# Two fused blocks on one core: the second block's first two tiles from undivided x, scans ahead of taps, one weight pass in four parts

## What is computed

```python
# end of the first block
x = x + ga2 * ((silu(gate) * up) @ w_down)
x = rmsnorm(x, g_final)
# the second block
h = rmsnorm_2(x, norm_g) * (1 + scale) + shift
cv, cg, cs, lx, ls = split(h @ w_in)          # 5 times 1024 columns
v = cv * sigmoid(cg)
v = causal_depthwise_conv(v, dw_w, dw_b)      # 31 taps a channel
v = silu(layernorm(v, cln_g, cln_b)) @ pw2_w + pw2_b
y_conv = v * silu(cs)
xs = causal_depthwise_conv(lx, sc_w, sc_b)    # 4 taps a channel
r = sigmoid(xs @ wr + br); i = sigmoid(xs @ wi + bi)      # by head
a = exp(-8 * r * softplus(-lam)); bx = sqrt(1 - a * a) * (i * xs)
hs = linear_scan(a, bx)                       # h = a h + bx along the tokens
x = x + (1 + gate) * (concat([y_conv, hs * silu(ls)]) @ w_out)
out = rmsnorm_2(x, final_g)
```

## Time and profile before

| | us |
|---|---|
| median of 3 runs | 1064.8 (1064.68 to 1064.96) |
| the profiled execution | 1064.87 |
| its span in the profile | 1063.1 |
| busy: TensorE | 1037.2 (98%) |
| busy: VectorE | 629.8 (59%) |
| busy: GpSimd | 471.5 (44%) |
| busy: ScalarE | 421.6 (40%) |
| mean granted TensorE clock | 0.998 |

### The profile page before, as it was taken

The page is one execution under the profiler, slowest core; times in us unless marked ns, Lnnn a source line. Parts: engine busy times, 40 slices in busy tenths (PEclk is TensorE's granted clock), DMA queues, the critical chain, the costliest instruction groups (busy, mean ns, idle before and its releaser), DMA issues.

```text
span 1063.1 us, 14023 instructions
## 1 busy us (share of the span) xinstructions
PE 1037.2 (98%) x5222; PEld 836.4 (79%) x5222; DVE 629.8 (59%) x1223; ACT 421.6 (40%) x585; POOL 471.5 (44%) x173
## 2 busy tenths in 40 slices
PE   6999999999999999999999999999999999999997
PEld 5787796667878888888888888888887777888886
DVE  5367997776463432224347100779999999664322
ACT  4244325883242222122242312424526777362242
POOL 0034343592333443534434444256865666734350
PEclk9999999999999999999999999999999999999999
DMA  9984231140424345343473323224231222322312
GB/s 325 349 288 126 73 117 40 41 160 1 158 80 158 118 133 178 124 157 119 133 237 124 109 85 105 80 80 158 79 119 40 79 80 80 119 80 93 105 40 80
DMA packets 127250, 128.91 MB, mean 121 GB/s; under 512 B 3552, under 2 KB 125280, under 8 KB 127200
## 3 DMA queue, kind: packets, MB, share of 16 engines
q1 hardware_dynamic: 125952, 127.38, 37.0%
q10 hardware_dynamic: 1248, 0.86, 0.3%
HBM read 126.13 MB, written 2.10 MB: 121 GB/s over the span
## 4 chain that ended last, share of the span: by engine, by line
PE 45%; issue 35%; POOL 14%; ACT 2%; SPq 1%; DMA 1%; DVE 1%; POOLq 0%; DVEq 0%; ACTq 0%
POOL w_lo L589 12%; PE bank L704 9%; PE bank L706 9%; PE bank L705 9%; PE bank L1021 2%; PE bank L1050 2%; PE bank L893 2%; PE bank L1245 1%; PE bank L1246 1%; PE bank L1244 1%; DMA ada_stage<-in_w_ada 1%; POOL lru_lo L682 1%; PE bank L911 1%; PE bank L729 1%; PE bank L730 1%
## 5 line engine op out<-in xcount | busy, mean ns | idle before, releaser
L589 POOL TENSOR_TENSOR w_lo<-w_stage,w_hi 128x2048 fp32r<-128x2048 f32 x78 | 371.5, 4762 | 500.4 <-ACT w_hi L1315 500.4
L704 PE MATMUL bank<-act_hi,w_hi 128*128 128x512 f32 x848 | 335.3, 395 | 1.2 <-POOL w_lo L589 1.1
L705 PE MATMUL bank<-act_lo,w_hi 128*128 128x512 f32 x848 | 330.0, 389 | 0.0
L706 PE MATMUL bank<-act_hi,w_lo 128*128 128x512 f32 x848 | 330.0, 389 | 0.0
L1315 ACT ACTIVATE w_hi<-w_stage 128x2048 fp32r<-128x2048 f32 x78 | 149.3, 1915 | 247.3 <-PE bank L706 236.1
L704 PEld LDWEIGHTS bank<-act_hi,w_hi 128*128 128x128 f32 x848 | 159.3, 188 | 40.1 <-issue 5.6
L706 PEld LDWEIGHTS bank<-act_hi,w_lo 128*128 128x128 f32 x848 | 159.2, 188 | 33.5
L705 PEld LDWEIGHTS bank<-act_lo,w_hi 128*128 128x128 f32 x848 | 159.3, 188 | 33.1 <-issue 1.2
L2156 DVE SCALAR_TENSOR_TENSOR bank<-v_pad,vcol,bank 128x512 f32<-128x512 f32 x208 | 138.1, 747 | 0.0
L2068 DVE TENSOR_TENSOR tmp<-bank,tmp 128x512 f32<-128x512 f32 x22 | 15.2, 692 | 157.1 <-PE bank L706 153.6
L704 PE MATMUL bank<-ff_hi,w_hi 128*128 128x512 f32 x176 | 69.7, 396 | 0.0
(11 more groups left out here) (316 smaller groups left out, 1548.1 us busy)
## 6 DMA issues: line engine op xcount, KB each, us to landing
w_stage<-in_w_in SPq DMA_DIRECT2D x29, 1024.0 KB, 5.1
w_stage<-in_w_gu SPq DMA_DIRECT2D x22, 1024.0 KB, 5.1
ada_stage<-in_w_ada SPq DMA_DIRECT2D x20, 1024.0 KB, 11.6
w_stage<-in_w_out SPq DMA_DIRECT2D x12, 1024.0 KB, 5.1
ada_stage<-in_mod_w SPq DMA_DIRECT2D x12, 1024.0 KB, 7.6
w_stage<-in_w_down SPq DMA_DIRECT2D x8, 1024.0 KB, 5.3
late_stage<-in_w_ada SPq DMA_DIRECT2D x4, 1024.0 KB, 9.4
w_stage<-in_pw_w SPq DMA_DIRECT2D x4, 1024.0 KB, 5.1
```

What stands on the lines that cost most here:

```text
L589: nc.gpsimd.tensor_tensor(w_lo[b][:], w_stage[b][:], w_hi[b][:].bitcast(F32), ALU.subtract).then_inc(s_lo, 1)
L704: pe.matmul(dst, wh, rhs_hi(k), start=(first and k == 0), stop=False)
L705: pe.matmul(dst, wh, rhs_lo(k), start=False, stop=False)
L706: mm = pe.matmul(dst, wl, rhs_hi(k), start=False, stop=(last and k == n_k - 1))
```

## The change

*Undivided tiles.* After each residual tile ScalarE makes `act_hi` and VectorE `act_lo` of xT times `scale1`, without the norm and the shift; TensorE runs the first chunk's two tiles on them, partly between the square sums. VectorE multiplies the two results by the inverse norm, and a sigmoid adds the bias row: the shift times the weights of that chunk, summed by VectorE over k (`bias_rows`) and by TensorE over the partitions, 128 columns at a time. The normed parts are still made, for the third tile on, and each waits until its undivided part is used. The sum of the square rows takes bank 2 in place of 0, and the filler matmuls there go.
*First block's output.* The eight VectorE products by g_final and the norm go; ScalarE copies the spread norm to SBUF, multiplies xT by g_final, and GpSimd by the norm, two tiles behind each of four chunks.
*Taps.* `TAPS_B` 10, 10, 10, 18 become 6, 6, 6, 10.
*w_lo in four.* Chunk C_OUT+1's pass is four passes over 512 columns each.
Beside these, SP waits for the bias rows before it loads chunk C_IN2+2 (they read the stage), and some semaphores are shared.

```diff
-TAPS_A, TAPS_B = (10, 10, 10, 10), (10, 10, 10, 18)
+TAPS_A, TAPS_B = (10, 10, 10, 10), (6, 6, 6, 10)
...
+            w_dma(C_IN2, w_cols(a["w_in_2"], 0, KD, D))
+            w_dma(C_IN2 + 1, w_cols(a["w_in_2"], 0, KD, 0))
+            sp.wait_ge(s_adaacc, len(ADA_ORD) + 1)
...
+            def lo_quarters(n, b):
+                pool.wait_ge(s_hi, n + 1)
+                for q in range(4):
+                    ks = slice(2 * q, 2 * q + 2)
+                    i = nc.gpsimd.tensor_tensor(w_lo[b][:, ks, :], w_stage[b][:, ks, :], w_hi[b][:, ks, :].bitcast(F32), ALU.subtract)
+                i.then_inc(s_lo, 1)
...
+                if n == C_OUT + 1:
+                    lo_quarters(n, n % 2)
+                    continue
...
+                if n in (C_IN2 + 4, C_IN2 + 6, C_IN2 + 8, C_IN2 + 10):
+                    for k in range(n - C_IN2 - 4, n - C_IN2 - 2):
+                        pool.wait_ge(s_x1g, k + 2)
+                        nc.gpsimd.tensor_tensor(xT[:, k, :], xT[:, k, :], cgate[:, 0, :], ALU.mult).then_inc(s_x1, 1)
...
                 if meanwhile:
                     meanwhile()
+                    if gained:
+                        spread(6, 7)
                     if spreads_back:
                         spread(4, 5)
                     return
                 keep_warm(WARM_COLUMNS, idle)
-                if gained:
-                    spread(6, 7)
...
+                        if (m2, g, m) == (KD // 2 - 1, 2, 0):
+                            pe.wait_ge(s_adaacc, len(ADA_ORD) + 1)
+                            for c in range(2):
+                                mm = pe.matmul(bank[7][:, NCOL + c:NCOL + c + 1], ada2_acc[:, c * P:(c + 1) * P], ones[:, 0:1],
+                                               start=True, stop=True)
+                            mm.then_inc(s_adamm, 1)
+            def undivided(ks):
+                for k in ks:
+                    pe.wait_ge(s_rawlo, k + 1)
+                    for dst, cols, ready in ((bank[0][:], low, s_i2acc), (bank[1][:], high, s_wused)):
...
+            def first_undivided():
+                pe.wait_ge(s_lo, C_IN2 + 1)
+                pe.wait_ge(s_res, 2 * KD - 2)
+                undivided((0, 1))
+
+            square_sums(gained=True, before=first_undivided, meanwhile=lambda: undivided((2, 3)))
+            undivided(range(4, KD))
             pe.wait_ge(s_res, 2 * KD)
             pe.wait_ge(s_lo, C_IN2 + 2)
-            abreast(third, 2, range(KD // 4))
-            abreast(two, 2, range(KD // 2, KD))
-            abreast(third, 2, range(KD // 4, KD))
-            tile(bank[3][:], b1, high, KD, hi, lo).then_inc(s_wused, 1)
+            abreast([(bank[2][:], b1, low, s_i2acc), (bank[3][:], b1, high, s_wused)], 2)
...
+                    if held and k < KD - 1:
+                        act.wait_ge(s_rawused, k + 1)
+                    elif held:
+                        act.wait_ge(s_wused, C_IN2 + 1)
...
+            def undivided_high(k):
+                if k == 0:
+                    act.wait_ge(s_mod, 11)
+                nc.scalar.activation(act_hi[:, k, :], xT[:, k, :], ACT.Copy, scale=scale1[:, 0, k:k + 1]).then_inc(s_rawhi, 1)
...
+                if j == 1:
+                    act.wait_ge(s_spread, 4)
+                    nc.scalar.activation(cgate[:, 0, :], bank[4][:], ACT.Copy).then_inc(s_x1g, 1)
+                    for k in range(KD):
+                        act.wait_ge(s_u, 2 * KD + k + 1)
+                        nc.scalar.activation(xT[:, k, :], xT[:, k, :], ACT.Copy, scale=col("g_final", k)).then_inc(s_x1g, 1)
...
+                            if j == 0:
+                                act.wait_ge(s_div, m + 1)
+                                act.wait_ge(s_mod, 12)
+                                nc.scalar.activation(tmp[m][:], tmp[m][:], ACT.Sigmoid, bias=first_bias[:, m:m + 1]).then_inc(s_sig, 1)
+                                continue
...
+            def bias_rows():
+                dve.wait_ge(s_stage[C_IN2 % 2], C_IN2 // 2 * 16 + 16)
+                for t in range(KD):
+                    src, w, part = w_stage[C_IN2 % 2][:, t, :], modc(SH3 + t), bank[7][:, 0:NCOL]
...
+                    if gained and k == KD - 2:
+                        bias_rows()
+                    if gained and k == KD - 1:
+                        dve.wait_ge(s_adamm, len(ADA_ORD) + 1)
+                        V.tensor_copy(first_bias[:], bank[7][:, NCOL:NCOL + 2]).then_inc(s_mod, 1)
                     if k >= 1:
                         add_squares(k - 1, gained)
+                    if gained and k >= 1:
+                        dve.wait_ge(s_rawhi, k)
+                        V.scalar_tensor_tensor(act_lo[:, k - 1, :], xT[:, k - 1, :], scale1[:, 0, k - 1:k],
+                                               act_hi[:, k - 1, :].bitcast(F32), ALU.mult, ALU.subtract).then_inc(s_rawlo, 1)
...
             normed(0, SH3, bank[6], (5, 7))
-            dve.wait_ge(s_spread, 4)
-            dve.wait_ge(s_u, 3 * KD)
-            for k in range(KD):
-                V.scalar_tensor_tensor(xT[:, k, :], xT[:, k, :], col("g_final", k), bank[4][:], ALU.mult, ALU.mult).then_inc(s_x1, 1)
-
+            link(V.tensor_copy(rstd[:], bank[6][:]))
+            for m in range(2):
+                dve.wait_ge((s_i2acc, s_wused)[m], (1, C_IN2 + 1)[m])
+                V.tensor_tensor(tmp[m][:], bank[m][:], rstd[:], ALU.mult).then_inc(s_div, 1)
```

More of the change, by code:

```diff
@@ L313, in build @@
         s_adaloop = sem("ada_loop_loaded")
-        s_late_ada = [sem(f"late_ada_loaded{b}") for b in range(len(ADA_LATE))]
         s_adastep = sem("ada_step")
@@ L337, in build @@
         s_sdg = sem("gained_deviation_ready")
+        s_rawhi = sem("undivided_hi_ready")
+        s_rawlo = sem("undivided_lo_ready")
+        s_rawused = sem("undivided_parts_used")
+        s_div = sem("first_tiles_divided")
         s_rc = sem("inverse_columns_ready")
@@ L561, in _ @@
                     late_dma(2 * n - 2)
-            stream(C_IN2, 4, [lambda j: w_cols(a["w_in_2"], 0, KD, j * NCOL + (D - NCOL)),
-                              lambda j: w_cols(a["w_in_2"], 0, KD, j * NCOL - NCOL)], first=1)
+            w_dma(C_IN2, w_cols(a["w_in_2"], 0, KD, D))
+            w_dma(C_IN2 + 1, w_cols(a["w_in_2"], 0, KD, 0))
+            sp.wait_ge(s_adaacc, len(ADA_ORD) + 1)
+            stream(C_IN2 + 2, 3, [lambda j: w_cols(a["w_in_2"], 0, KD, j * NCOL + (D - NCOL)),
+                                  lambda j: w_cols(a["w_in_2"], 0, KD, j * NCOL - NCOL)], first=2)
             for g in range(2):
@@ L752, in sums @@
                     return mm
-                plain = 0 if gained else 6
+                plain = 2 if gained else 6
                 if gained:
@@ L1172, in _ @@
                             late_products(b)
-            square_sums(gained=True)
+                        if (m2, g, m) == (KD // 2 - 1, 2, 0):
[4 more added lines that the diff above has]
+                            mm.then_inc(s_adamm, 1)
+            b0, b1 = C_IN2 % 2, (C_IN2 + 1) % 2
+            def undivided(ks):
+                for k in ks:
+                    pe.wait_ge(s_rawlo, k + 1)
+                    for dst, cols, ready in ((bank[0][:], low, s_i2acc), (bank[1][:], high, s_wused)):
+                        wh, wl = w_hi[b0][:, k, cols], w_lo[b0][:, k, cols]
+                        pe.matmul(dst, wh, act_hi[:, k, :], start=(k == 0), stop=False)
+                        pe.matmul(dst, wh, act_lo[:, k, :], start=False, stop=False)
+                        mm = pe.matmul(dst, wl, act_hi[:, k, :], start=False, stop=(k == KD - 1))
+                        if k == KD - 1:
+                            mm.then_inc(ready, 1)
+                    if k < KD - 1:
+                        mm.then_inc(s_rawused, 1)
+            def first_undivided():
[4 more added lines that the diff above has]
+            undivided(range(4, KD))
             pe.wait_ge(s_res, 2 * KD)
-            b0, b1 = C_IN2 % 2, (C_IN2 + 1) % 2
-            pe.wait_ge(s_lo, C_IN2 + 1)
-            two, third = [(bank[0][:], b0, low, s_i2acc), (bank[1][:], b0, high, s_wused)], [(bank[2][:], b1, low, s_i2acc)]
-            abreast(two, 2, range(KD // 2))
             pe.wait_ge(s_lo, C_IN2 + 2)
-            abreast(third, 2, range(KD // 4))
-            abreast(two, 2, range(KD // 2, KD))
-            abreast(third, 2, range(KD // 4, KD))
-            tile(bank[3][:], b1, high, KD, hi, lo).then_inc(s_wused, 1)
+            abreast([(bank[2][:], b1, low, s_i2acc), (bank[3][:], b1, high, s_wused)], 2)
             with pe.Fori(1, KD // 2) as j:
@@ L1362, in squares, with act_hi_parts @@
                 act.wait_ge(s_col, j)
-                nc.scalar.activation(cols[:, 4, :], first_of_block(bank[0 if gains else 6]), ACT.Sqrt, bias=eps[:, 0:1], scale=1.0 / D).then_inc(s_sd, 1)
+                nc.scalar.activation(cols[:, 4, :], first_of_block(bank[2 if gains else 6]), ACT.Sqrt, bias=eps[:, 0:1], scale=1.0 / D).then_inc(s_sd, 1)
             splits = [0]
```

(12 more changed lines are left out.)

13 lines of the change are left out of this document (12 added, 1 removed).

## The result

The changed kernel took 1066.65 us (median of 20 runs, 1065.6 to 1068.23) against 1064.87 for the kernel before beside it (20 runs): ratio 1.0015, 95% interval 1.0009 to 1.0022. The forecast was 1061.2, its range 1058.6 to 1064.2: the time lies 5.4 us above the forecast and 2.4 above the range. The profiled execution took 1066.31 us, its span is 1064.5, the mean granted clock 0.995 (0.998 before). It is read here against the 1064.87 of the profile before.

The account below looks back on a forecast made before the run. TensorE, busy nearly all the span, was taken to set the end, so only its waits or needless work could pay. Terms -1.78 + 0.5 + 0.85 - 3.2 = -3.6 took 1064.87 to 1061.2 us, range 1058.6 to 1064.2.

Parts of the forecast that it names:

- w_lo in four parts, -1.78: Attention stretch: the inverse_wide copy gets in between GpSimd's four shorter passes, so TensorE gains 1.78 us.
- The fifth rival: Attention stretch: GpSimd runs all four w_lo parts without letting VectorE in; 1.78 less gained, 1063.0 us, chance 0.08.
- Bias matmuls, +0.5: Hinge between the blocks: the bias row's one-column matmuls cost TensorE 0.5 us ahead of the undivided tiles.
- Third chunk, +0.85: Hinge: w_lo of the third chunk comes late, TensorE idles some 4.2 us and starts that chunk 0.85 us later.
- g_final on ScalarE and GpSimd: Last two GpSimd products collide with VectorE's short conv at 783; VectorE 1.5 us later, TensorE loses 1.5 us.
- the stage's -3.2: Recurrent stage: 4.7 us gained by earlier scans, less 1.5 lost to the GpSimd products, gives 3.2 us.
- Scans ahead of taps, -4.7: Recurrent stage: scans come 2.64, 5.28 and 7.92 us earlier, so TensorE's waits on gates and w_lo go, 4.7 us.
- VectorE's cover at the mean sums: End of the recurrent stage: 2 to 3 us of VectorE's 9.6 us ahead of TensorE's mean sums are left.
- Rivals 2 and 3: Clock falls in the hinge's 4.2 us gap, 1062.7; GpSimd's pass at 813 goes first, blocking VectorE, 1064.2; chance 0.14 each.
- The fourth rival: Hinge: the clock falls in the gap and half rate lasts; 12 us of it costs 6, 1067.2 us, chance 0.06.
- A rule weighed: At 813.74: the trace shows one engine standing still meanwhile, but not that each turn on the shared port is one instruction.

Follow-up runs that it names:

- kernel with 13 taps: Kernel before with TAPS_A = (13, 10, 10, 10) and TAPS_B = (7, 10, 10, 18), so VectorE reaches its run of SBUF operations three taps later: 1069.26 us.
- products one later: Changed kernel with the last two GpSimd products of xT one chunk later, behind the w_lo pass that follows them: 1066.92 us.
- early split: Changed kernel with ScalarE's split of the third chunk ahead of its two sigmoids, right behind act_hi: 1060.67 us.

## Why the prediction was wrong

By its own steps:

- **w_lo in four parts, -1.78.** Right. The copy took 1.43 us (about 1.2 foreseen), and the run with this alone gave 1.6. The fifth rival is out.
- **Bias matmuls, +0.5.** Right: from 661.81 to 662.18 they take 0.37 us, and the matmul behind them comes 0.1 late, 0.46 together.
- **Third chunk, +0.85.** The mechanism was right, and the gap with it (4.2 foreseen, 4.13 measured); quarters, bias and this together are -0.25 where the sum had -0.43. What was mis-sized is the term's other half, which I left to a rival: the clock. The gap lowered it here and in every other profiled kernel that has this gap unfilled, four others. In the kernel with the products two chunks later it fell within the gap already, at 0.50 from 696.9 to 703.7, and `v_pad` came at 722.74, 1.1 us later than in the changed kernel. From the start of the third chunk to `v_pad`, against the kernel before, it costs 1.5 to 2.8 us in the five. Filling the gap gave 2.2. I gave this 0.14 and 1 to 2 us; the place was right, the size about right, and five profiles out of five speak against so low a chance.
- **g_final on ScalarE and GpSimd: "I take 1.5 ... So TensorE loses 1.5 us".** This is the step that failed. The collision was there and no less than foreseen (11.53 against 9.46, 2.07 us; 1.34 of it came back at the two operations of L2238, 1.41 us where 2.75 were taken before, so that VectorE was 0.73 late at 815 with respect to the pass; both were also late with TensorE). But its price is not proportional. It spent a lead of 0.11 us, which I put at 0.7 because I compared the pass's 813.74 with the start of the whole stretch (812.7, the TENSOR_SCALAR pair) and not with the first operation of the run that shuts the pass out (813.63). With that row read, the flip is no rival of 0.14 but the forecast: any lateness over 0.11 us brings it. Even by the prediction's own two numbers, 1.5 us late with 0.7 us in hand, the pass would have come first; that VectorE kept it out before was no reason against it, since VectorE was then the first. What the runs showed in place of the 1.5 is the pass at 4.72 us with VectorE blocked, and the stage's -3.2 of the sum measured as +0.06 (from +1.38 at `v_pad` to +1.44 at the mean sums), the second fall of the clock in it. With the lead won back by the order of the taps alone the time was 4.7 us less.
- **Scans ahead of taps, -4.7.** Right, and a little low: alone 5.1, in the changed kernel 5.2. It is the only reason why the changed kernel is 1.8 us slower and not 7.
- **VectorE's cover at the mean sums.** 2 to 3 us foreseen, 2.33 measured.

Rivals 2 and 3 are what happened, both, and the flip's new gap (2.17 us) brought a second fall of the clock, about 1.7 us. I had given each its own chance as if one excluded the other; but the clock at the hinge and the race at 815 have nothing to do with each other, and the third even makes a case of the second. Worked out together from my own figures: 1064.87 - 1.78 + 0.5 + 0.85 - 0.2 = 1064.2 for the flip, and two falls of 1.5 make 1067.2. The profiled execution had 1066.31. The fourth rival, one fall that lasts, gave that time as well and is wrong about how: both half rates of the changed kernel lasted 3.4 us, and none with work at hand in any other profile more than 6.8.

**A rule weighed.** The Trainium skill (SBUF — State Buffer, section "SBUF: two separate sides") has whoever starts first hold the shared pair for one whole instruction. For GpSimd's pass the traces agree: VectorE stands for all of its 4.6 us, and gets in between two parts of a pass that is split. For VectorE they show two things. In the race, where the pass comes after 7.8 to 10.3 us in which GpSimd was idle, it is kept out by the unbroken run of two-input operations and not by one of them; eight profiles have it, with leads of 0.10 to 1.33 us. But where GpSimd's instructions follow each other without a break, the two engines take turns one instruction at a time. The kernel before has such a place (GpSimd's timeline), within the run of six of 777.09:

```profile
778.29 5.06 POOL L589 TENSOR_TENSOR w_lo<-w_stage,w_hi 128x2048 fp32r<-128x2048 f32 x1
```

This pass is 0.46 over 4.6: it stood aside for the first of the six operations only, and the second waited for it. The collision of the changed kernel is the same. The pass of 779.65 took 5.05, and the two products of 784.66 took 1.75 each in place of 1.29, each with one operation of VectorE ahead of it. So the prediction's reading, that the trace doesn't show each turn to be one instruction, was true of 813.74 and not of 778.29. What makes the difference, the idle time ahead of the pass or something else, no run here isolates.

**Open.** Why the clock falls behind the 2.2 us gap in some executions (the changed kernel, and the one with filler at the hinge; in the kernel with 13 taps behind one of 2.42 and again behind one of 1.86) and not in others (products one later, 2.21; early split, 2.18; 1.81 in the kernel before) no run here tells. It wasn't tried to fill that gap.

## What to carry to other kernels

Where two engines meet on a resource that one of them holds for a run of instructions, find in the trace the two starts that decide who is first, and write down the lead with its sign. A cost that only uses up slack elsewhere is a step function there: 0.11 us of lead were worth 4.7 us. And before an edit that trades busy time of TensorE for a gap of some microseconds, price the gap at the clock's rate as well, or put filler or the work that it waits for into it first: moving one ScalarE operation 3.6 us up took 6.0 us off this kernel.
